# Rotations and a row spread as two products of rounded parts instead of one float32 product

## The reference, cut to what matters

```python
def apply_axial_rope(x, cos, sin):          # A: q and k, after rms_norm
    ...
    out = jnp.stack([x1 * cc - x2 * ss, x2 * cc + x1 * ss], axis=-2)

q = apply_axial_rope(rms_norm(q, q_g), cos, sin)
...
# mLSTM, one chunk
logD = a[..., :, None] - a[..., None, :] + li[..., None, :]
inter = a + m[..., None]
m_t = jnp.maximum(inter, jnp.max(logD, axis=-1))
s = jnp.einsum('bhld,bhsd->bhls', qc, kc) * jnp.exp(logD - m_t[..., None])
...
def _partial_rope(u, pos):                  # sparse attention: q, k
    ...
    r1 = u1 * cos - u2 * sin
    r2 = u2 * cos + u1 * sin
q_rope = _partial_rope(nq, positions)
```

## Time and profile before

| | |
|---|---|
| runs | 1618.10, 1622.68, 1623.65 us; median 1622.68 |
| profiled execution, its own time | 1619.39 us |
| its span | 1617.7 us |
| mean granted clock of PE | 0.98 |
| busy PE | 1540.9 us (95%) |
| busy DVE | 752.5 us (47%) |
| busy ACT | 640.4 us (40%) |
| busy POOL | 685.8 us (42%) |
| DMA | 128.23 MB, mean 79 GB/s |

### The profile page before, as it was taken

One profiled execution on the slowest core, in us unless ns is written; L12 is line 12 of the kernel. 1 busy time (PEld: TensorE's weight loads), 2 busy tenths in 40 slices (PEclk: granted clock), 3 DMA queues, 4 the chain that ended last, 5 costly groups with the idle time before them and its releaser, 6 DMA issues.

```text
span 1617.7 us, 25534 instructions
## 1 busy us (share of the span) xinstructions
PE 1540.9 (95%) x10050; PEld 1235.7 (76%) x10050; DVE 752.5 (47%) x1743; ACT 640.4 (40%) x1345; POOL 685.8 (42%) x661
## 2 busy tenths in 40 slices
PE   5899999999899999999998899999999989999997
PEld 3777777777587888787876677878787867766877
DVE  4434555554533534444355454733433564455154
ACT  3334444444531533333334363434332344444331
POOL 2534344443432533433335345435355434444462
PEclk8999999999999999999998899999999999999998
DMA  9121011110123222222231222212121221111221
GB/s 396 36 76 52 30 52 53 53 53 27 53 94 116 79 72 85 105 79 88 97 105 43 88 85 79 79 56 101 52 95 61 83 102 53 53 53 53 82 93 60
DMA packets 23142, 128.23 MB, mean 79 GB/s; under 512 B 2416, under 2 KB 4592, under 8 KB 9072
## 3 DMA queue, kind: packets, MB, share of 16 engines
q1 hardware_dynamic: 22880, 126.35, 22.1%
q10 hardware_dynamic: 144, 0.26, 0.1%
HBM read 124.50 MB, written 2.10 MB: 78 GB/s over the span
## 4 chain that ended last, share of the span: by engine, by line
PE 83%; DVE 8%; ACT 3%; POOL 2%; issue 2%; DMA 1%; SPq 0%; POOLq 0%; DVEq 0%; ACTq 0%
PE PS L1477 16%; PE PS L1479 16%; PE PS L1478 16%; PE PS L1557 7%; PE PS L1567 6%; PE PS L1592 6%; PE PS L1470 3%; PE PS L1471 3%; PE PS L1472 3%; DVE sm L2166 1%; PE PS L1645 1%; PE PS L1637 1%; PE PS L1490 1%; DMA XC<-in_xt 1%; DVE AR L2082 1%
## 5 line engine op out<-in xcount | busy, mean ns | idle before, releaser
L2493 POOL TENSOR_TENSOR WL<-W,WH 128x512 fp32r<-128x512 f32 x304 | 400.7, 1333 | 325.1 <-ACT WH L1748 324.7
L1477 PE MATMUL PS<-HX,WH 128*128 128x512 f32 (+1 forms) x1040 | 426.2, 410 | 11.5 <-DVE LX L2087 3.7
L1479 PE MATMUL PS<-HX,WL 128*128 128x512 f32 (+1 forms) x1040 | 404.2, 389 | 0.0
L1478 PE MATMUL PS<-LX,WH 128*128 128x512 f32 (+1 forms) x1040 | 403.7, 388 | 0.0
L1477 PEld LDWEIGHTS PS<-HX,WH 128*128 128x128 f32 x1040 | 199.3, 192 | 60.5 <-issue 17.5
L1479 PEld LDWEIGHTS PS<-HX,WL 128*128 128x128 f32 x1040 | 198.2, 191 | 41.3
L1478 PEld LDWEIGHTS PS<-LX,WH 128*128 128x128 f32 x1040 | 199.0, 191 | 34.5 <-issue 2.6
L1748 ACT CAST WH<-W 128x512 fp32r<-128x512 f32 x320 | 186.8, 618 | 37.2 <-PE PS L1472 21.1
L1834 ACT ACTIVATE AR<-PS,sm 128x768 f32<-128x768 f32 (+4 forms) x160 | 115.5, 722 | 163.8 <-DVE sm L2171 93.7
L2166 DVE TENSOR_REDUCE sm<-PS 128x1 f32<-128x512 f32 (+4 forms) x224 | 150.0, 670 | 54.3 <-PE PS L1557 49.7
L2560 POOL TENSOR_SCALAR AR<-AR,sm 128x768 f32<-128x768 f32 (+1 forms) x96 | 74.8, 780 | 186.5 <-DVE sm L2182 186.5
(11 more groups left out here) (285 smaller groups left out, 2537.6 us busy)
## 6 DMA issues: line engine op xcount, KB each, us to landing
W<-in_wu SPq DMA_DIRECT2D x98, 1024.0 KB, 4.8
AR<-in_wu SPq DMA_DIRECT2D x8, 1024.0 KB, 11.6
AR<-in_biasb SPq DMA_DIRECT2D x32, 256.0 KB, 2.7
XX<-in_xt SPq DMA_DIRECT2D x2, 1024.0 KB, 6.0
XC<-in_xt SPq DMA_DIRECT2D x1, 1024.0 KB, 14.4
out<-XX SPq DMA_DIRECT2D x2, 512.0 KB, 3.0
out<-XX SPq DMA_DIRECT2D x4, 256.0 KB, 2.2
C<-in_cc SPq DMA_DIRECT2D x1, 770.5 KB, 8.5
```

The costliest lines, as they stand in the source:

```text
L1477: e.matmul(o, wh, xh, start=(k == 0), stop=False)
L1478: e.matmul(o, wh, xl, start=False, stop=False)
L1479: t = e.matmul(o, wl, xh, start=False, stop=(k == 7))
L2493: e.tensor_tensor(WL[:, d, a:z], W[:, n % 2, a:z], WH[:, d, a:z].bitcast(F32), ALU.subtract).then_inc(*s_wl_pool.by(n, q))
```

## The change

- `rotations`: ACT casts the two constant matrices to fp32r into a new tile PM, once, after the second part of the key work.
- A: `query_parts` casts the query on ACT (L1798) into ARp and subtracts on DVE (L2094), right behind `query_sums`. `a_query_turn` is now two fp32r products, of the high and the low part, and waits for the low part in place of the query. It moves from k=3 to k=5 of the gate group, `query_rope` from k=6 to k=7; for pair 0 the turn moves from between the value projections into the gate group, behind k=3.
- mLSTM: `row_parts`, after the last value of head 0: ACT casts the selectors and, when it is there, `nM`; DVE subtracts. `m_exp` is two fp32r products.
- Sparse attention: `rotate_parts` behind each `n_query`: cast on ACT (L1798), subtraction on POOL (L2534). `n_rotate` of a query is two fp32r products; the two keys' stay float32. The high parts lie in the places of `kx`, so `n_cmp_in` waits for the rotation of query m+2.

The products high x matrix and low x matrix stand for the whole product, since the matrices hold only 0, 1 and -1.

```diff
+        PM = sb("PM", [P, 256], F32R)
+        rot1, rot2 = PM[:, 0:128], PM[:, 128:256]
...
+        HIGH["q"] = Blocks(*[ARp[:, 17664:18176]] * 8)
+        LOW["q"] = Blocks(ARp[:, 13824:14336], *[ARp[:, 12288:12800]] * 7)
+        HIGH["r"] = Blocks(*[ARp[:, a:a + T] for a in (15872, 16384, 15872, 16384)])
+        LOW["r"] = Blocks(ARp[:, 10240:12288])
+        selr, nM_h, nM_l = ARp[0:4, 17920:18432], ARp[0:4, 15424:15936], ARp[0:4, 16448:16960]
...
+        def query_parts(pair):
+            after = [(s_qsum, (pair,)), (s_qraw, (pair, 1))] + ([(s_qrot, (pair - 1,))] if pair else [])
+            parts("q", pair, 0, qT[pair % 2][:, 0:T], after, "dve")
...
-                yield from gate_group(pair, 0, FX, {2: lambda: query_sums(pair, FC), 3: lambda: query_turn(pair, FC), 6: lambda: query_rope(pair)})
+                yield from gate_group(pair, 0, FX, {2: lambda: (query_sums(pair, FC), query_parts(pair)), 5: lambda: query_turn(pair, FC), 7: lambda: query_rope(pair)})
...
         key_work[1]()
+        do("rotations")
...
         query_sums(0, vr)
+        query_parts(0)
         values((4,))
-        query_turn(0, vr)
         values((5,))
         unv.done(s_proj, "av", 5)
-        run(gate_group(0, 0, vr))
+        run(gate_group(0, 0, vr, {3: lambda: query_turn(0, vr)}))
...
+            if hd == 0:
+                do("row_parts")
             do_later(hd)
...
+        def rotate_parts(key, src, by):
+            n = rotas[key] = len(rotas)
+            free_by = (s_nrot, (("q", n - 2),)) if n >= 2 else (s_den, (3,))
+            parts("r", n, 0, src, [by, free_by], "pool")
...
             def a_query_turn(pair):
                 free(w, ("aqr", pair))
-                w.wait_ge(*s_qraw(pair, 1))
-                e.matmul(aqps[pair, "rot"], c("p1"), qT[pair % 2][:, 0:T], start=True, stop=True).then_inc(*s_qrot.by(pair))
+                w.wait_ge(*s_pm())
+                w.wait_ge(*s_xl_dve("q", pair, 0))
+                o = aqps[pair, "rot"]
+                e.matmul(o, rot1, high("q").at(pair, 0, T), start=True, stop=False)
+                e.matmul(o, rot1, low("q").at(pair, 0, T), start=False, stop=True).then_inc(*s_qrot.by(pair))
...
-                w.wait_ge(*s_nM())
-                e.matmul(mps["E", hd], selv[0:4, hd, :], nM, start=True, stop=True).then_inc(*s_eb.by(hd))
+                w.wait_ge(*s_selr())
+                w.wait_ge(*s_nMl())
+                sel = selr[:, 128 * hd:128 * hd + 128]
+                e.matmul(mps["E", hd], sel, nM_h, start=True, stop=False)
+                e.matmul(mps["E", hd], sel, nM_l, start=False, stop=True).then_inc(*s_eb.by(hd))
...
+            def row_parts():
+                e.copy(selr, c("sel")[0:4]).then_inc(*s_selr.by())
+                w.wait_ge(*s_nM())
+                e.copy(nM_h, nM).then_inc(*s_nMh.by())
...
             def n_cmp_in(m):
                 w.wait_ge(*s_proj("nc", m))
+                w.wait_ge(*s_nrot(("q", m + 2)))
...
+            def row_parts():
+                w.wait_ge(*s_nMh())
+                e.tensor_tensor(nM_l, nM, nM_h.bitcast(F32), ALU.subtract).then_inc(*s_nMl.by())
```

More of the change, by code:

```diff
@@ L297, in build @@
         s_mz = signal("m_zero")
-        s_gi, s_gf, s_gr, s_fa, s_em, s_gth, s_sin, s_cos = shared("m_set_up_act", 8)
-        s_fl, s_F, s_g, s_nM, s_nS, s_gc, s_gb, s_gt, s_tb, s_tb2 = shared("m_set_up_dve", 10)
+        s_gi, s_gf, s_gr, s_fa, s_em, s_gth, s_sin, s_cos, s_pm, s_selr, s_nMh = shared("m_set_up_act", 11)
+        s_fl, s_F, s_g, s_nM, s_nS, s_gc, s_gb, s_gt, s_tb, s_tb2, s_nMl = shared("m_set_up_dve", 11)
         s_gt1, s_gt2, s_gt3 = shared("gcol_turned", 3)
@@ L1122, in build @@
         em3 = em.rearrange("p (j h) -> p j h", j=4)
-        selv = c("sel").rearrange("p (h n) -> p h n", h=4)
         C2, S2 = CS[:, 0:T], CS[:, T:2 * T]
@@ L1249, in build @@
                     pend.pop()()
+                rotate_parts(("q", m), qr[:, m, :], (s_nq, (m,)))
                 pend.append(lambda m=m: rotate(("q", m), qr[:, m, :], (s_nq, (m,)), qp[:, m, :]))
@@ L1675, in n_rotate @@
                 free(w, ("nrot", key))
-                w.wait_ge(*ev(*k))
-                e.matmul(o, c("p2"), src, start=True, stop=True).then_inc(*s_nrot.by(key))
+                n = rotas.get(key)
+                if n is None:
+                    w.wait_ge(*ev(*k))
+                    e.matmul(o, c("p2"), src, start=True, stop=True).then_inc(*s_nrot.by(key))
+                else:
+                    w.wait_ge(*s_xl_pool("r", n, 0))
+                    e.matmul(o, rot2, high("r").at(n, 0, T), start=True, stop=False)
+                    e.matmul(o, rot2, low("r").at(n, 0, T), start=False, stop=True).then_inc(*s_nrot.by(key))
             def n_hidden(m, i):
@@ L1792, in low_ctx_k, with rotations @@
                 e.activation(h, h, ACT.Identity, bias=shift, scale=scale_).then_inc(*s_scaled_act.by(l, k))
+            def rotations():
+                w.wait_ge(*s_c())
+                e.copy(PM[:, :], c("p1", 0, 256)).then_inc(*s_pm.by())
+            def row_parts():
+                e.copy(selr, c("sel")[0:4]).then_inc(*s_selr.by())
+                w.wait_ge(*s_nM())
+                e.copy(nM_h, nM).then_inc(*s_nMh.by())
             def parts(phase, k, j):
@@ L2003, in scalar @@
             program(e, w, dict(silu=silu, split=split, mod_row=mod_row, square=square, scale_ctx=scale_ctx, scale_ctx_k=scale_ctx_k, low_ctx_k=low_ctx_k, scale=scale,
+                               rotations=rotations, row_parts=row_parts,
                                parts=parts, a_key_raw=a_key_raw, a_key_rope=a_key_rope, a_query_raw=a_query_raw, a_gate=a_gate, score_exp=score_exp,
@@ L2475, in vector @@
             program(e, w, dict(silu=silu, split=split, mod_tr=mod_tr, square=square, norm_rs=norm_rs, norm2_rs=norm2_rs, rbroad=rbroad,
-                               gain=gain_, scale=scale, scale_low=scale_low, parts=parts, a_key_raw=a_key_raw, a_value=a_value, a_key_sums=a_key_sums,
+                               row_parts=row_parts, gain=gain_, scale=scale, scale_low=scale_low, parts=parts, a_key_raw=a_key_raw, a_value=a_value, a_key_sums=a_key_sums,
                                a_key_norm=a_key_norm, a_key_rope=a_key_rope, a_query_raw=a_query_raw, a_query_sums=a_query_sums,
```

2 lines of the change are left out of this document (1 added, 1 removed).

## The result

| | before | changed |
|---|---|---|
| runs | 20 | 20 |
| median | 1620.24 us | 1623.79 us |
| lowest to highest | 1614.97 to 1623.65 | 1620.94 to 1628.09 |
| profiled execution, its span | 1617.7 us | 1621.8 us |

The ratio is 1.0022, with a 95% interval of 1.0014 to 1.0030: some 3.6 us slower. The forecast was 2.0 us faster. The time is inside the range that was given, but it moved the other way, beyond its interval; the prediction was wrong. Ratios in this document are of fast runs; four slow ones, of 1756 to 2919 us, two of them of the kernel before, are left out.

What follows compares the result with a forecast made beforehand. PE's queue plus its few waits was taken as the bound. Block A +0.5, mLSTM -1.6 and sparse queries -0.9 sum to -2.0 us: 1620.7 us against the median of 1622.68, range 1615.8 to 1626.5.

Steps and rivals of the forecast that it cites:

- The saving on PE: Two rounded products replace each float32 one: 0.43 us less per call, 6.9 us over 16 calls if nothing waits.
- mLSTM's spreads: mLSTM: four spreads save 0.43 us each, 1.7 in all, less 0.1 of waiting: -1.6 us.
- third rival: All rotations and spreads: the new products are as dear as the old, +4.9 us, 1627.6 us; chance 0.03.
- Pair 0: Block A, before attention starts: the later turn meets no wait, so the whole saving stays, -0.43 us.
- Pairs 2 to 4: Block A: the rope row comes later and swallows PE's saving, +0.3 us each, +0.9 in sum.
- Pairs 5 and 6: Block A: savings less short waits for the subtraction or a later rope, -0.1 us and -0.2 us.
- Pair 1: Block A: POOL's multiplication L2553 comes 0.90 later and nothing is given back, +0.9 us.
- Pair 7: Block A: longer waits for rope and exponential, the 1.90 wait gone: -0.6 us, bounds -1.4 and +1.0.
- The sparse queries: Sparse attention: 1.7 us saved, less waits for POOL's parts at q2 and q3: -0.9 us, bounds -1.7 and +0.3.
- second rival: Block A, pairs 2 to 5: DVE's subtraction stands still during POOL's power, +2.8 us in all, 1625.5 us; chance 0.24.
- first rival: Whole kernel: the row behind the pairs is looser, nothing waits, 6.9 us go, 1615.8 us; chance 0.20.

Runs made afterwards that it cites:

- both mends: Whole change, with POOL's cosine multiplication moved right behind the parts and sparse query q2 left in float32, against the kernel before: ratio 0.9934, median 1610.80 us.

## Why the prediction was wrong, point by point

- **The saving on PE** was right where nothing waits. The mLSTM's spreads give 0.37 each (0.43 forecast), q0 and q1 0.42 each. The third rival (products no cheaper) falls.
- **Pair 0**, forecast -0.4, fits as far as the trace can tell: behind it the changed kernel is 1.06 ahead, of which 0.7 was there at 77 us, before its turn.
- **Pairs 2 to 4** were right: +0.26 for +0.3 each, with the addition at 0.69. The kernel that only moves the turn has the same +0.26, so the pairs' own savings are swallowed, as forecast. **Pairs 5 and 6** gained 0.2 and 0.35 for 0.1 and 0.2.
- **Pair 1**, forecast +0.9, was +2.8. Up to the wait the term was near (1.24 grew to 2.65, that is 1.2 more on the way out of it); 0.3 of it is the addition that took 1.67 and not 1.32, where I had written that nothing is given back and not that something is added. What failed is that every term was priced at the full clock of the earlier trace rows. Behind the wait the clock fell, for another 1.6.
- **Pair 7**, forecast -0.6 with bounds of -1.4 and +1.0, was +2.0 (1.98 to 3.95). The step that failed is "the step's scores wait 0.5 to 1.0 more for the rope": they wait 2.0 more. I had counted how much later the turn stands on PE, and not what POOL does with it: the rope starts 0.8 later, measured from where the kernel is, and takes 0.8 longer beside a split. The lower clock behind the wait adds some 0.8. The two effects behind it (the 1.90 gone, the exponential at 1.88) came as told.
- **The sparse queries**, forecast -0.9, came to about +2. The sum for the rotations was right: q0 and q1 gain 0.42 each, q2 and q3 nothing (the difference is 1.20 behind q1 and 1.14 behind q3), so their two savings went into waiting for POOL's parts, as forecast. The trace books only 0.19 of that as idle; the rest shows in the starts. The step that failed is "nothing is put down for it", on the splits behind the subtractions. POOL does catch up, but a weight load is issued from a split's end, and it kept the whole delay for 40 us. That cost 1.2, about the 1.27 that I had put in the bound. The other 1.5 are the clock from 1303 us on, which kernels without this wait lose too.
- **What I had no term for:** 1.2 behind pair 7 up to 578.7 (a lower clock at two places), and 1.6 gained near 1095, where only the kernel before has a low clock. That the time still came out inside the range is luck: the range reached up to a microsecond over the second rival's time, and this rival didn't happen.
- **The second rival** (the subtraction stands still during the power) fell: it took 0.69 us in each of the seven pairs where it lies inside the power. It had named the right sign and, by accident, nearly the right size (+2.8), by a wrong mechanism. By the Trainium skill ("SBUF — State Buffer", section "SBUF: two separate sides") the GpSimd instruction would hold the shared ports for its whole length, and the subtraction would have had to wait. This case doesn't agree with it for a power over 12 columns; beside splits over 512 columns (1.75 to 1.78 for 0.69, ending behind the split) it does.
- **The first rival** (nothing waits, -6.9) fell: PE's waits for the value row went from 3.9 to 6.1 us.

What stays open is the lower clock. A long wait and a fall behind it go together in most cases, in the kernel before too: between 100 and 1320 us it has seven waits of PE of over 2 us, and behind six of them the next 4 us have a mean granted clock of 0.62 or less; in the changed kernel it is nine of nine. But the length of the wait doesn't decide. The moved kernel's 2.50 in pair 1 had no fall behind it, nor had the 2.39 at 429.4 us of the kernel before, while the moved kernel's 2.40 at the same place had one. And the same wait of 1.90 at the same product was followed by no fall in the kernel before (upper two lines) and by one in the kernel with pairs 1 and 7 as before (lower two). Each first line is from a timeline, as in the earlier trace rows, each second one a window, as in the earlier trace rows:

```profile
415.54 1.07 PE L1490 MATMUL PS<-W,sm 128*32 128x256 f32 x16 [1.90 <-DVE AR L2146]
416.00:420.00 4.00, 3.83 (x35) 2.07 (x27) 1.28 (x3) 0.50 (x2) 0.56 (x1) 1.00 0.56 184
```

```profile
415.08 1.22 PE L1509 MATMUL PS<-W,sm 128*32 128x256 f32 x16 [1.90 <-DVE AR L2188]
416.00:420.00 4.00, 4.00 (x21) 2.19 (x19) 0.21 (x1) 0.38 (x1) 0.10 (x1) 0.59 0.64 223
```

That the two falls cost the changed kernel 1.6 us and some 0.8 is read from the traces; that the waits cause them is likely and not shown: no run here was made to set the clock apart from the waits.

How much of the measured times goes with the clock can be estimated from the runs. Over 81 runs of the kernel before, made beside the experiments, time and mean granted clock go together (correlation -0.90), 0.83 us for each 0.001 of clock. The changed kernel has a mean of 0.9743 for 0.9770. By that line 2.2 of the 3.2 us between the two means go with the clock, and 1.0 (+-0.4) is left at the same clock. Of both mends' 10.6 us (0.9818 for 0.9752) about 5.4 go with the clock and 5.2 are left. So part of what was measured seems to be how much time each kernel spends at the lower clock, and a sum at the full clock has no term for that.

## What to carry to other kernels

A step that is moved later on the busiest engine must be followed on every in-order queue that it takes part in: here POOL's place in pair 1 cost PE a wait of 2.65, and taking that one instruction forward turned block A from 3.7 us slower to 1.9 faster. When work goes into the queue of an engine with time to spare, ask what is *released* by the instruction behind it, above all a load, which keeps a delay that the engine itself makes up. Rounded parts are copies, so once they are made their source is free: look for what no longer has to wait.

## What the runs showed of the hardware

- Two fp32r products of 128x512 in place of one float32 product save 0.37 to 0.42 us at the full clock where nothing waits (0.37 where the product has 4 rows).
- On DVE, a subtraction or addition with two 128x512 inputs in SBUF took 0.69 beside POOL's power over 12 columns (2.28 us long), 1.66 to 1.79 beside splits (1.27 for one alone).
- In the 4 us behind a wait of 2.65 us the trace has 24 of PE's products, where the kernel before, at the full clock, has 40. A wait of 1.90 us at the same product was followed by a clock of 0.59 in one kernel and of 1.00 in another.
- Over 81 runs of one kernel the times lie between 1615 and 1626 us, and they follow the mean granted clock (0.971 to 0.982).
